# Two gates and two key projections regrouped into seven half-size products, and a scan begun on half its stacks

## Chip, cores and metric

The kernel runs on one core of one Trainium2 chip, in float32 throughout. The metric is the device time of one execution in microseconds (us), lower is better.

## What is computed

Two transformer blocks, one after the other, on 256 tokens of 1024 channels. The first mixes three branches (latent attention, gated linear attention, attention to a memory), each weighed by a gate, and ends in a feed-forward. The second mixes a state space branch and a dilated attention. Cut to what matters here:

```python
# first block
proj = rms_norm(x, g_mix) @ w_in                     # the last 3 * 1024 columns are gate_logits
gates = sigmoid(gate_logits + b_gate).reshape(B, S, 3, 1024)
y = gates[..., 0, :] * o_mla + gates[..., 1, :] * o_gla + gates[..., 2, :] * o_mem
x = x + y @ w_o
# second block: u_s, z_s, q, k, v, z_a, r_s, r_a = columns of rms_norm(x) @ w_in_2
q = rope(rms_norm(q))    # three groups of 512 columns, one per dilation
k = rope(rms_norm(k))    # the same
y_s = state_space(u_s)   # a scan along the tokens
y_a = dilated_attention(q, k, v)
m = sigmoid(r_s) * (...y_s...) + sigmoid(r_a) * (...y_a...)
```

## The kernel before

Every engine's program is written out by hand as one list. An engine does its list in order, and a semaphore wait holds back all that stands behind it on that engine.

**Jobs.** A projection of 512 columns is a job: both tiles of 128 tokens (its two halves), eight 128x128 by 128x512 products each. One such product is two MATMUL instructions in the trace. `fill` cuts a job into four parts of four products, to be laid between other work. Outputs take turns in two pairs of PSUM banks: before an output's first product TensorE waits until the output two places earlier has been taken out (`taken`, lines 195 to 204 and `half_job`).

**Groups of seven.** A projection of 1024 columns over 1024 channels can be a group (`GROUPS`): seven products of quarter blocks, Q1 to Q7, in place of eight, each four 128x512 products (`group_multiply`, L2028 and L2032). In exchange VectorE forms sums: four of the rows (`group_rows`; the row sums are shared where two groups have the same input), four of the weights, 128x2048 each (`group_t1`, `group_t3`, `group_t2`, `group_t4`), and five combinations of results (`group_z`, `group_v`, `group_c12`, `group_c22`, `group_last`). ScalarE copies Q1 and Q5 (`group_copy`) and takes out the first block (`group_first`). Of the waits: Q2 waits for the copy of Q1, Q6 for the third weight sum (T2), Q4 for the fourth (T4) and for `group_z`. The semaphore `first_out` counts `group_c12`; it stands for the first of a group's two PSUM pairs in `taken`.

**Weights** come through a ring of three 2 MB slots, loaded on SyncE's queue in the order of the jobs; a slot is freed by the last product that reads it (for a group: Q7 frees the first half's slot, Q4 the second's).

**The stretch of the gates** (L2156 on). After the latent attention, TensorE does products 2, 7, 3 of group MV (the memory's values), turns the normalised queries and keys of the memory attention (`turn`, L1892), does MV's Q6, waits for ScalarE to have taken the turned keys out (`is_turned("km")`), and enters a loop of nine steps. A step lays two parts of the gate jobs (in step 0 MV's Q4) ahead of: the memory attention's scores (L2167), their transposes, its values (L2183), and the lane products of one level of the gated linear attention (L2199). VectorE's step takes the scores and the values, takes the level's products, makes the decayed queries and keys and the exponents of the next level (`level_diff`), and from step 3 on takes and applies gates.

**The scan** (L2388 on). `us0` and `us1` of the state space branch come out of PSUM by ScalarE, VectorE stacks them with 16 copies (L1683), and eight steps of `drive` (L2381), VectorE's scan and `states` follow, with parts of eight jobs (`early`) between them.

**The dilated attention's queries and keys.** `dq0` to `dq2` and `dk0` to `dk2` are six jobs. Each goes through ScalarE (a copy and a square, L850 and L852), VectorE (`dqk`: sums, root, norm, rotation) and a transpose on TensorE. One buffer, `raw`, serves all six. Then come the groups RS, RA (the two output gates) and GLU, and the attention itself: `pair_scores` (L2444), VectorE's maxima (L1206), ScalarE's exponentials (L708), with eighths of RA and GLU laid between.

Of the kernel before, what the change touches and what calls it, by code (L numbers as in the profile page):

```python
# [12 lines left out]
P = 128  # L13
# [26 lines left out]
CH = 128  # L40
# [42 lines left out]
RG, MV, UP = 3, 4, 5  # L83
RS = UP + 4
# [4 lines left out]
def jobs_table():  # L89
# [13 lines left out]
    j = [(f"gate{i}", "w_in", C_GATE + 512 * i, 512) for i in (0, 1, 4, 5, 2, 3)]  # L103
# [10 lines left out]
    j += [(f"dk{g}", "w_in_2", C_DK + DW * g, DW) for g in range(NDIL)]  # L114
    out += [(n, n, w, 0, DM, c, m) for n, w, c, m in j]
    out += halves(RS, C_RS, "w_in_2") + halves(RA, C_RA, "w_in_2") + halves(GLU, 0, "w_glu_2")
# [10 lines left out]
ORDERS[UP] = ORDERS[WP] = (1, 2, 5, 7, 3, 6, 4)  # L127
# [3 lines left out]
ROWS = (0, 1, 1, 2, 3) + 4 * (4,) + (5, 5, 6, 7, 8)  # L131
# [6 lines left out]
for _job in JOBS:  # L138
# [10 lines left out]
BY_DVE = {"gg", "wo0", "wo1", "ao0", "ao1"} | {f"gate{i}" for i in range(6)}  # L149
# [30 lines left out]
    "dqk_rows": "one group's queries or keys of the dilated attention",  # L180
    "angle": "reduced rotary angles", "rope_ready": "ScalarE: cosines and sines",
# [19 lines left out]
    "u_ready": "state space inputs, even and odd steps stacked", "u2_ready": "halves of those stacks",  # L201
# [28 lines left out]
def act_at(i, n):  # L230

    return 3 * i + n - max(i - SO, 0)
# [12 lines left out]
def build(nc, d, out):  # L245
    with ExitStack() as ctx:
# [79 lines left out]
        sum_t2 = [r_gla, r_gla, r_gla, arena[:, dec_at:dec_at + 2048], arena[:, dec_at:dec_at + 2048]]  # L326
        sum_t3 = arena[:, r_at + 2048:r_at + 4096]
        sum_rows = [knT, mem_tok, mem_tok, arena[:, dec_at + 2048:dec_at + 4096], arena[:, dec_at + 2048:dec_at + 4096]]
# [47 lines left out]
        assert a4.at <= work_at  # L376
        tail_q1, tail_q5 = arena[:, 7680:8192], arena[:, 16384:16896]
        tail_t2 = {RS: m_tok, RA: sig_glu, GLU: m_tok, SO: arena[:, work_at:work_at + 2048], WP: arena[:, work_at + 4096:work_at + 6144]}
        rows_raw = arena[:, work_at + 6144:work_at + 8192]
        tail_rows = {RS: zs, RA: zs, GLU: rows_raw, SO: arena[:, work_at + 2048:work_at + 4096], WP: rows_raw}  # L380
# [25 lines left out]
        def group(i):  # L406
# [5 lines left out]
            if i < RS:  # L412
                t2, t3 = (x.rearrange("p (k n) -> p k n", n=512) for x in ((sum_t2[i], sum_t3) if i < UP else (up_t2, up_t3)))
                if i in (RG, MV):
                    t3 = b12
# [9 lines left out]
        def temporaries(i):  # L425
            if i >= RS:
                return tail_q1, tail_q5, tail_q5, tail_q1
            if i == MV:
                return copied_q1, across, across, copied_q1
            return (copied_q1, copied_q5, sum_z, sum_v) if i < UP else (up_q1, up_q5, up_z, up_v)  # L430
# [2137 lines left out]
```

## Time and profile before

| | us |
|---|---|
| median of 3 runs | 970.54 (969.59 to 970.54) |
| the profiled execution, whole | 969.14 |
| its span from first to last instruction | 967.2 |
| TensorE matmul, busy | 954.4 |
| VectorE, busy | 697.0 |
| ScalarE, busy | 220.4 |

The span leaves out some 1.9 us at the ends of the execution. All times in the views below are counted from the span's start. A line such as L928 is a helper that records all of VectorE's two-operand instructions, so operations are told apart by shape and place in time, not by line. In the chain of waits matmuls are shown from the end of the one before, in the timeline from their own issue, some 0.15 us earlier.

### The profile page before, as it was taken

How to read it: one execution, taken by the hardware profiler on the slowest of the kernel's cores; microseconds unless marked ns; L12 is line 12 of the kernel's file. 1: busy time of each engine (PE TensorE's matmuls, PEld its weight loads, DVE VectorE, ACT ScalarE, POOL GpSimd, SP SyncE). 2: the span in 40 equal slices, each digit the busy share in tenths (PEclk: the TensorE clock that was granted, in tenths of full speed). 3: DMA queues.
4: the chain of work that ended last, by engine and by line, in shares of the span. 5: the costliest groups of instructions: out<-in, count | busy, mean ns of one | idle time of the engine just before them, and what ended most of it. 6: DMA issues, size and time to landing. Idle time of an engine off the chain costs nothing.

```text
span 967.2 us, 12513 instructions
## 1 busy us (share of the span) xinstructions
PE 954.4 (99%) x5014; PEld 590.6 (61%) x5014; DVE 697.0 (72%) x1259; ACT 220.4 (23%) x438; POOL 23.2 (2%) x27
## 2 busy tenths in 40 slices
PE   7999999999999999999999999999999999999998
PEld 6944445754555449999844469458854444468544
DVE  4866964586566887866899763888965969674667
ACT  4313422223241232422200011001011321434200
POOL 0000000000002500000000000000000000000000
PEclk9999999999999999999999999999999999999999
DMA  9551731443345624344454443425243434321631
GB/s 329 149 196 43 283 130 44 174 134 128 97 158 155 182 109 169 115 175 175 174 174 173 174 149 124 164 88 175 87 138 124 173 116 150 109 105 45 218 130 44
DMA packets 53818, 139.76 MB, mean 144 GB/s; under 512 B 3968, under 2 KB 7904, under 8 KB 53760
## 3 DMA queue, kind: packets, MB, share of 16 engines
q1 hardware_dynamic: 52304, 135.07, 39.7%
q0 software_dynamic: 1248, 3.80, 1.7%
q8 instruction: 40, 0.66, 0.3%
q14 instruction: 18, 0.15, 0.0%
q10 hardware_dynamic: 208, 0.08, 0.0%
HBM read 137.90 MB, written 1.05 MB: 144 GB/s over the span
## 4 chain that ended last, share of the span: by engine, by line
PE 92%; DVE 5%; ACT 1%; issue 1%; DMA 0%; DVEq 0%; ACTq 0%
PE pair L1947 36%; PE pair L2032 18%; PE pair L2028 16%; PE pair L2286 6%; PE turned L1892 4%; PE score L2286 3%; DVE arena L928 3%; PE turned L2286 1%; PE score L2381 1%; PE score L2457 1%; PE score L2131 1%; PE score L2444 1%; PE score L2183 1%; PE score L2130 1%; PE score L2199 1%
## 5 line engine op out<-in xcount | busy, mean ns | idle before, releaser
L1947 PE MATMUL pair<-ring,hT 128*128 128x512 f32 (+2 forms) x640 | 269.8, 576 | 0.9 <-ACT hT L600 0.9
L928 DVE TENSOR_TENSOR arena<-arena 128x512 f32<-128x512 f32 (+6 forms) x329 | 194.1, 604 | 13.4 <-PE score L2286 4.1
L1947 PEld LDWEIGHTS pair<-ring,hT 128*128 128x128 f32 x640 | 119.2, 190 | 130.5 <-issue 125.5
L1947 PE MATMUL pair<-hT,ring 128*128 128x128 f32 (+2 forms) x464 | 76.4, 324 | 0.2 <-ACT hT L600 0.2
L928 DVE TENSOR_TENSOR arena<-pair,arena 128x512 f32<-128x512 f32 x57 | 39.4, 691 | 46.6 <-PE pair L2032 22.7
L2032 PE MATMUL pair<-ring,arena 128*128 128x512 f32 x160 | 71.7, 594 | 0.0
L1947 PEld LDWEIGHTS pair<-hT,ring 128*128 128x128 f32 (+1 forms) x464 | 66.0, 188 | 9.0 <-issue 1.3
L928 DVE TENSOR_TENSOR arena<-ring 128x2048 f32<-128x2048 f32 (+1 forms) x37 | 67.7, 1831 | 2.5 <-DMA ring<-in_w_ssm_out 1.3
L2032 PE MATMUL pair<-arena 128*128 128x512 f32 x144 | 65.3, 595 | 0.3 <-DVE arena L928 0.3
L2028 PE MATMUL pair<-arena 128*128 128x128 f32 x544 | 64.0, 276 | 0.0
L2032 PE MATMUL pair<-ring,hT 128*128 128x512 f32 x136 | 62.4, 598 | 0.8 <-DMA ring<-in_w_in 0.8
L2028 PEld LDWEIGHTS pair<-arena 128*128 128x128 f32 x544 | 62.2, 192 | 0.3 <-issue 0.2
L571 ACT ACTIVATE arena<-turned 128x512 f32<-128x512 f32 (+2 forms) x66 | 32.7, 536 | 129.2 <-PE turned L1892 129.2
L2028 PE MATMUL pair<-hT,ring 128*128 128x128 f32 x480 | 55.7, 275 | 0.0
L2028 PEld LDWEIGHTS pair<-hT,ring 128*128 128x128 f32 x480 | 54.7, 192 | 0.7 <-issue 0.5
L1892 PEld LDWEIGHTS turned<-ident,arena 128*128 128x128 f32 (+1 forms) x363 | 41.1, 141 | 22.2 <-issue 16.5
L1892 PE MATMUL turned<-ident,arena 128*128 128x128 f32 (+1 forms) x363 | 49.8, 275 | 1.7 <-ACT arena L571 0.7
L2032 PEld LDWEIGHTS pair<-ring,arena 128*128 128x128 f32 x160 | 29.7, 190 | 34.6 <-issue 34.6
L1206 DVE CUSTOM_DVE_ANT_0 arena<-score,masks 128x256 f32<-128x256 f32 (+2 forms) x40 | 18.0, 451 | 42.4 <-PE score L2131 22.1
L2032 PEld LDWEIGHTS pair<-arena 128*128 128x128 f32 x144 | 26.8, 190 | 32.0 <-issue 31.3
L2286 PE MATMUL pair<-ring,arena 128*128 128x512 f32 x96 | 43.5, 592 | 0.0
L928 DVE TENSOR_TENSOR arena<-arena,ring 128x2048 f32<-128x2048 f32 (+1 forms) x22 | 41.9, 1904 | 1.6 <-PE pair L2028 0.6
(221 smaller groups left out, 1004.4 us busy)
## 6 DMA issues: line engine op xcount, KB each, us to landing
ring<-in_w_in SPq DMA_DIRECT2D x33, 2048.0 KB, 8.4
ring<-in_w_up SPq DMA_DIRECT2D x8, 2048.0 KB, 8.5
ring<-in_w_down SPq DMA_DIRECT2D x8, 2048.0 KB, 7.8
ring<-in_w_o SPq DMA_DIRECT2D x4, 2048.0 KB, 7.9
ring<-in_w_mem_kv SPq DMA_DIRECT2D x2, 2048.0 KB, 7.8
ring<-in_w_glu SPq DMA_DIRECT2D x2, 2048.0 KB, 7.8
ring<-in_w_ssm_out SPq DMA_DIRECT2D x2, 2048.0 KB, 7.8
ring<-in_w_ukv SPq DMA_DIRECT2D x4, 512.0 KB, 3.7
```

The costliest lines, as they stand in the source:

```text
L571: act.activation(dst, src, ACT.Copy).then_inc(sem("turned_taken"), 1)
L928: return dve.tensor_tensor(o, a, b, op)
L1206: ins = dve.tensor_tensor_reduce(dst, src, mask, scale, -3e38, ALU.add, ALU.max, st[:, a:a + 1])
L1892: ins = pe.transpose(b[0:x.shape[1], a:a + rows], x, ident[0:rows, 0:rows])
L1947: ins = pe.matmul(o_, s, m, start=a, stop=b)
L2028: ins = pe.matmul(h[bank_][:, P * c:P * c + P], weights[:, k, P * c:P * c + P], rows[:, k, :], start=not onto and c == 0 and k == 0, stop= ...
L2032: ins = pe.matmul(h[bank_], rows[:, k, :], weights[:, k, :], start=not onto and k == 0, stop=k == 3, skip_group_check=True)
L2130: pe.matmul(o, qnT[:, SEQ * h + P * t:SEQ * h + P * t + P], knT[:, SEQ * h:SEQ * h + w], start=True, stop=False)
L2131: ins = pe.matmul(o, qpT[r, SEQ * (h // 2) + P * t:SEQ * (h // 2) + P * t + P], kpeT[r, 0:w], start=False, stop=True)
L2183: ins = pe.matmul(b[:, SEQ * t:SEQ * t + SEQ], s[:, 256 * t + P * k:256 * t + P * k + P], vm3[:, k, EV * h:EV * h + EV], start=k == 0, sto ...
L2199: ins = pe.matmul(b[lane0:lane0 + w, w * x:w * x + w], ks[:, P * x + k0:P * x + k0 + w], qs[:, P * x + q0:P * x + q0 + w], start=True, sto ...
L2286: ins = pe.matmul(product[q], rows[:, k, :], weights[:, k, :], start=g == 0 and k == 0, stop=g == 7 and k == 1, skip_group_check=True)
```

## The change

One more group, GT, takes the place of the jobs `gate0` and `gate1`, and one, DK, that of `dk1` and `dk2`.

- GT: its row sums are formed in step 8 of the attention before (`group_rows(GT)`); its seven products stand in steps 0 to 3 of the loop, its weight sums at the start of step 0 (T1), in step 1 (T3, T2), at the end of step 2 (T4 and `group_z`), and its last results at the end of step 3. Bias is added while the blocks are taken out. Both gates get one sigmoid and one multiplication.
- DK: seven products after `dk0`. Its row sums also serve RS and RA, whose own are gone. Two buffers, `raws`, take the place of `raw`; squares of the last two groups' keys are taken by ScalarE out of SBUF, and both share one root.
- The scan: of the 16 stacking copies VectorE keeps the first eight; ScalarE does the others. `drive(0)` moves ahead of the first two parts of `early`, and `states(7)` ahead of two parts at the end.

Of the diff, the parts that move work (further lines set buffers, names and places of temporaries; `stacks` lists the source and target of the eight copies of one half; `temporaries(GT)` and `(DK)` give their own scratch; `dqk_squares` and `dqk_turn` are `dqk` cut in two):

```diff
@@ -100,7 +101,8 @@
     out += [("mq", "mq", "w_in", 0, DM, C_MQ, 256), ("mk", "mk", "w_mem_kv", 0, DM, 0, 256)] + halves(MV, 256, "w_mem_kv")
-    j = [(f"gate{i}", "w_in", C_GATE + 512 * i, 512) for i in (0, 1, 4, 5, 2, 3)]
+    out += halves(GT, C_GATE)
+    j = [(f"gate{i}", "w_in", C_GATE + 512 * i, 512) for i in (4, 5, 2, 3)]
@@ -111,8 +113,9 @@
     j += [(f"dq{g}", "w_in_2", C_DQ + DW * g, DW) for g in range(NDIL)]
-    j += [(f"dk{g}", "w_in_2", C_DK + DW * g, DW) for g in range(NDIL)]
+    j += [("dk0", "w_in_2", C_DK, DW)]
     out += [(n, n, w, 0, DM, c, m) for n, w, c, m in j]
+    out += halves(DK, C_DK + DW, "w_in_2")
@@ -124,11 +127,11 @@
 ORDERS = {i: (1, 5, 2, 7, 3, 6, 4) for i in range(NG)}
-ORDERS[UP] = ORDERS[WP] = (1, 2, 5, 7, 3, 6, 4)
+ORDERS[GT] = ORDERS[UP] = ORDERS[WP] = (1, 2, 5, 7, 3, 6, 4)
...
-ROWS = (0, 1, 1, 2, 3) + 4 * (4,) + (5, 5, 6, 7, 8)
+ROWS = (0, 1, 1, 2, 3, 4) + 4 * (5,) + (6, 6, 6, 7, 8, 9)
@@ -758,12 +780,21 @@
                     level_exp(i)
+                if i == 1:
+                    group_copy(GT, 5)
...
                     exps("mem", i, ((0, 256, 0), (256, 256, 1)))
-                if i in (4, 6, 8):
-                    gate_sigmoid((i - 4) // 2)
+                if i == 0:
+                    group_copy(GT, 1)
+                if i == 4:
+                    act.wait_ge(sem("first_out"), GT + 1)
+                    act.wait_ge(sem("second_out"), GT + 1)
+                    act.wait_ge(sem("last_out"), GT + 1)
+                    act.activation(gate_buf, gate_buf, ACT.Sigmoid).then_inc(sem("gate_sig"), 1)
+                if i == 8:
+                    gate_sigmoid(2)
@@ -816,6 +847,10 @@
                 ins.then_inc(sem("taken_act"), 1)
+            act.wait_ge(sem("taken_act"), taken("us1")[1])
+            for h, jj, s, src, dst in stacks(1):
+                ins = act.activation(dst, src, ACT.Copy)
+            ins.then_inc(sem("u2_late"), 1)
@@ -837,30 +872,43 @@
-            for n in range(6):
-                name = f"dq{n}" if n < 3 else f"dk{n - 3}"
-                act.wait_ge(sem("z_silu"), 3)
-                if n:
-                    for _k in range(2):
-                        turned((qdT if n - 1 < 3 else kdT)[:, 1024 * ((n - 1) % 3) + 512 * _k:1024 * ((n - 1) % 3) + 512 * _k + 512], 512)
-                if n == 0:
-                    act.wait_ge(sem("h_ready"), 4 * 8)
+            def turned_dqk(n):
...
+                for k in range(2):
+                    turned((qdT if n < 3 else kdT)[:, 1024 * (n % 3) + 512 * k:1024 * (n % 3) + 512 * k + 512], 512)
...
+            act.wait_ge(sem("z_silu"), 3)
+            act.wait_ge(sem("h_ready"), 4 * 8)
+            for n, name in enumerate(("dq0", "dq1", "dq2", "dk0")):
+                x, squares = raws[n % 2]
...
                 for t in range(2):
-                    act.activation(raw[:, 512 * t:512 * t + 512], p[:, 512 * t:512 * t + 512], ACT.Copy)
+                    act.activation(x[:, 512 * t:512 * t + 512], p[:, 512 * t:512 * t + 512], ACT.Copy)
                 for t in range(2):
-                    ins = act.activation(raw2[:, 512 * t:512 * t + 512], p[:, 512 * t:512 * t + 512], ACT.Square)
+                    ins = act.activation(squares[:, 512 * t:512 * t + 512], p[:, 512 * t:512 * t + 512], ACT.Square)
                 ins.then_inc(sem("taken_act"), 1)
-                if n == 2:
+                if n == 0:
...
                                        scale=1.5957691216057308).then_inc(sem("gelu_sig"), 1)
+                else:
+                    turned_dqk(n - 1)
+            group_copy(DK, 1)
+            group_copy(DK, 5)
+            turned_dqk(3)
+            group_first(DK, raws[1][0][:, 0:512])
+            act.wait_ge(sem("first_out"), DK + 1)
+            act.wait_ge(sem("second_out"), DK + 1)
+            act.activation(raws[0][1], raws[0][0], ACT.Square).then_inc(sem("dk_squared"), 1)
+            act.wait_ge(sem("group_act"), act_at(DK, 3))
+            act.wait_ge(sem("last_out"), DK + 1)
+            act.activation(raws[1][1], raws[1][0], ACT.Square).then_inc(sem("dk_squared"), 1)
...
             group_first(RS, by_tokens(rsig)[0])
-            for k in range(2):
-                turned(kdT[:, 2048 + 512 * k:2048 + 512 * k + 512], 512)
+            turned_dqk(5)
+            turned_dqk(4)
@@ -983,15 +1031,17 @@
                 weights_in(f"g{i}x")
-                if i and i != RA:
-                    dve.wait_ge(sem("group_product"), product_at(i - 1 if i != GLU else RS, 6))
+                if i == GT:
+                    dve.wait_ge(sem("group_product"), product_at(MV, 4))
+                elif 0 < i < DK or i in (SO, WP):
+                    dve.wait_ge(sem("group_product"), product_at(i - 1, 6))
...
                 weights_in(f"g{i}y")
-                if 0 < i < RS:
+                if 0 < i < DK:
@@ -1277,6 +1327,7 @@
                     m_squares(0)
+                    group_rows(GT)
@@ -1335,9 +1386,17 @@
             level_diff(0)
+            gt4 = by_tokens(gate_buf)
+            h, (_, _, z, v), biased = group(GT)[0], temporaries(GT), ckv[:, 0:512]
             for i in range(9):
+                if i == 0:
+                    group_t1(GT)
...
                     group_last(MV, vm4[2])
+                    group_t3(GT)
+                    dve.wait_ge(sem("bgate0"), 16)
+                    dve.wait_ge(sem("group_product"), product_at(GT, 2))
+                    link(tt(gt4[0], h[1], bgate[:, 0:512], ALU.add))
@@ -1387,10 +1446,25 @@
                         mark(dve.tensor_copy(am3[q, :, q], ad3[q]), "amat")
-                if i in (3, 5, 7):
-                    gate_take((i - 3) // 2)
-                if i in (5, 7):
-                    gate_apply((i - 5) // 2, (i - 5) // 2 + 1)
+                if i == 1:
+                    group_t2(GT)
+                if i == 2:
+                    group_t4(GT)
+                    group_z(GT)
+                if i == 3:
+                    group_v(GT)
+                    dve.wait_ge(sem("bgate1"), 16)
+                    link(tt(biased, v, bgate[:, 512:1024], ALU.add))
+                    dve.wait_ge(sem("group_product"), product_at(GT, 3))
+                    mark(tt(gt4[1], h[3], biased, ALU.add), "first_out")
+                    mark(tt(gt4[3], z, biased, ALU.add), "second_out")
+                    link(tt(v, v, bgate[:, 0:512], ALU.subtract))
+                    group_last(GT, gt4[2])
+                if i == 5:
+                    dve.wait_ge(sem("gate_sig"), 1)
+                    link(tt(o_mla, o_mla, gate_buf, ALU.mult))
+                if i == 7:
+                    gate_take(2)
@@ -1404,8 +1478,8 @@
             mark(tt(o_gla, o_gla, r_gla, ALU.mult), "mixer_out")
-            gate_apply(2, 3)
-            gate_apply(3, 4)
+            gate_apply(2, 2)
+            gate_apply(3, 3)
@@ -1672,16 +1749,18 @@
-            u4 = uT.rearrange("p (m c s) -> p m c s", c=CH, s=2)
-            v4 = u2.rearrange("p (m h c) -> p m h c", h=2, c=CH)
-            for i in range(2):
-                dve.wait_ge(sem("taken_act"), taken(f"us{i}")[1])
-                for h in range(2):
-                    for jj in range(2):
-                        for s in range(2):
-                            q, r = 64 * h + 32 * jj, 64 * jj + 32 * s
-                            ins = dve.tensor_copy(v4[r:r + 32, 4 * i:4 * i + 4, h, :], u4[q:q + 32, 4 * i:4 * i + 4, :, s])
-                            step(ins) if (h, jj, s) != (1, 1, 1) else mark(ins, "u2_ready")
+            def dqk(n):
...
+                x, squares = raws[n % 2]
+                dqk_squares(n, squares, 192)
+                mean(st[:, 192:208], st[:, 192:208], DD)
+                inverse_root(192, 16)
+                dqk_turn(n, x, squares, 208)
...
+            dve.wait_ge(sem("taken_act"), taken("us0")[1])
+            for h, jj, s, src, dst in stacks(0):
+                ins = dve.tensor_copy(dst, src)
+                step(ins) if (h, jj, s) != (1, 1, 1) else mark(ins, "u2_ready")
@@ -1721,31 +1800,42 @@
                     z_silu(("zs0", "zs1", "za")[m - 5])
-            dqk(0)
             ssm_out(7)
-            dqk(1)
...
                 mark(tt(z, z, y, ALU.mult), "gelu_z")
-            dqk(2)
+            dqk(0)
+            group_rows(DK)
...
                 link(tt(z, y, zs[:, 1024 * i:1024 * i + 1024], ALU.mult))
-            group_rows(RS)
+            dqk(1)
+            group_t1(DK)
+            dqk(2)
+            group_t3(DK)
             dqk(3)
+            group_t2(DK)
+            group_t4(DK)
             group_t1(RS)
-            dqk(4)
+            group_z(DK)
+            group_middle(DK, raws[0][0][:, 0:512], raws[0][0][:, 512:1024])
+            group_last(DK, raws[1][0][:, 512:1024])
             group_t3(RS)
-            dqk(5)
+            dqk_squares(5, raws[0][1], 192)
+            dqk_squares(4, raws[1][1], 208)
+            mean(st[:, 192:224], st[:, 192:224], DD)
+            inverse_root(192, 32)
+            dqk_turn(5, raws[0][0], raws[0][1], 224)
             group_t2(RS)
+            dqk_turn(4, raws[1][0], raws[1][1], 240)
...
             group_z(RS)
+            dve.wait_ge(sem("turned_ready"), T_DQK)
             group_t1(RA)
-            dve.wait_ge(sem("turned_ready"), T_DQK)
@@ -2156,10 +2246,13 @@
             for i in range(9):
-                if i:
-                    fill(["gate0", "gate1", "gate4", "gate5"], i - 1, 2)
+                if i < 4:
+                    for g, q in (((MV, 4), (GT, 1)), ((GT, 2), (GT, 5)), ((GT, 7), (GT, 3)), ((GT, 6), (GT, 4)))[i]:
+                        group_multiply(g, q)
+                elif i < 7:
+                    fill(["gate4", "gate5"], i - 4, 2)
                 else:
-                    group_multiply(MV, 4)
+                    fill(["gate4", "gate5"], i - 1, 1)
@@ -2388,18 +2481,20 @@
             pe.wait_ge(sem("ca_ready"), 2)
-            fill(early, 0, 2)
             for m in range(8):
-                if m in (0, 4):
-                    pe.wait_ge(sem("u2_ready"), m // 4 + 1)
+                if m == 0:
+                    pe.wait_ge(sem("u2_ready"), 1)
+                if m == 4:
+                    pe.wait_ge(sem("u2_late"), 1)
                 drive(m)
-                fill(early, 3 * m + 2, 1)
-                fill(early, 3 * m + 3, 1)
+                fill(early, 3 * m, 1)
+                fill(early, 3 * m + 1, 1)
...
                     states(m - 1)
-                fill(early, 3 * m + 4, 1)
+                fill(early, 3 * m + 2, 1)
+            fill(early, 12, 2)
+            states(7)
             fill(early, 13, 2)
-            states(7)
@@ -2407,19 +2502,26 @@
                 for k in range(2):
-                    turn(f"dqk{n}", ktiles(raw, DW)[4 * k:4 * k + 4])
+                    turn(f"dqk{n}", ktiles(raws[n % 2][0], DW)[4 * k:4 * k + 4])
             pe.wait_ge(sem("ssm_taken"), 8)
-            for n, name in enumerate(("dq2", "dk0", "dk1", "dk2")):
+            for n, name in enumerate(("dq2", "dk0")):
...
                 job(name)
+            turn_dqk(2)
+            for q in (1, 5, 2):
+                group_multiply(DK, q)
+            turn_dqk(3)
+            for q in (7, 3, 6, 4):
+                group_multiply(DK, q)
+            for q in (1, 5, 2, 7):
+                group_multiply(RS, q)
             turn_dqk(4)
-            for q in (1, 5, 2, 7):
+            for q in (3, 6):
...
             assert n_unit["turned"] == T_DQK, n_unit
-            for q in (3, 6, 4):
-                group_multiply(RS, q)
+            group_multiply(RS, 4)
...
             eighths = [0]
```

## Rows read from the trace of the kernel before

**Rows 1.** The page: busy time by engine, and the chain's shares by engine
```profile
PE 954.4 (99%) x5014; PEld 590.6 (61%) x5014; DVE 697.0 (72%) x1259; ACT 220.4 (23%) x438; POOL 23.2 (2%) x27
...
PE 92%; DVE 5%; ACT 1%; issue 1%; DMA 0%; DVEq 0%; ACTq 0%
```

**Rows 2.** Windows: stretch, busy time of each engine, clock, DMA share, GB/s
```profile
210.00:305.00 95.00, 95.00 (x692) 50.46 (x691) 62.01 (x108) 28.61 (x41) 1.61 (x3) 1.00 0.42 135
...
720.00:815.00 95.00, 95.00 (x295) 44.83 (x294) 70.46 (x144) 22.05 (x41) 0.00 (x0) 1.00 0.42 151
```

**Rows 3.** Chain of waits: a whole job; start, us, what
```profile
751.48 13.74 PE pair L1947 x32
```

**Rows 4.** Groups by form: VectorE's operations, busy us, mean ns
```profile
L928 DVE TENSOR_TENSOR arena<-arena 128x1024 f32<-128x1024 f32 x43 | 51.9, 1223 | 1.2
L928 DVE TENSOR_TENSOR arena<-ring 128x2048 f32<-128x2048 f32 x21 | 48.1, 2292 | 1.9 <-DMA ring<-in_w_ssm_out 1.3
...
L928 DVE TENSOR_TENSOR arena<-pair,arena 128x512 f32<-128x512 f32 x57 | 39.4, 691 | 46.6 <-PE pair L2032 22.7 <-PE pair L2028 17.1 <-PE pair L1947 5.5
```

**Rows 5.** Chain of waits: TensorE through steps 0, 2 and 3 of the loop
```profile
216.92 6.87 PE pair L2032 x16
223.78 1.06 PE score L2167 x4
224.84 0.69 PE score L2199 x50
...
245.76 0.63 PE score L2199 x32
...
256.82 0.69 PE score L2199 x50
```

**Rows 6.** Timeline, ScalarE: silu's sigmoid, turned queries and keys, exponentials
```profile
217.29 1.06 ACT L738 ACTIVATE arena<-arena 128x1024 f32<-128x1024 f32 x1 [9.22 <-DVE arena L928]
218.26 1.07 ACT L571 ACTIVATE arena<-turned 128x512 f32<-128x512 f32 x2
...
227.93 0.19 ACT L708 ACTIVATION_READ_ACCUMULATOR arena<-arena,stats 128x1 f32 x1
```

**Rows 7.** Timeline, VectorE: steps 0, 2 and 3 of the loop
```profile
199.27 2.29 DVE L928 TENSOR_TENSOR ring<-ring 128x2048 f32<-128x2048 f32 x1
...
225.89 0.42 DVE L1206 CUSTOM_DVE_ANT_0 arena<-score,masks 128x256 f32<-128x256 f32 x1
...
247.99 3.81 DVE L928 TENSOR_TENSOR arena<-arena 128x1024 f32<-128x1024 f32 x4
...
258.61 3.21 DVE L928 TENSOR_TENSOR arena<-arena 128x256 f32<-128x256 f32 x5
```

**Rows 8.** Timeline, VectorE: one of the keys' `dqk`, first scores of the dilated attention
```profile
783.50 1.22 DVE L1659 TENSOR_REDUCE stats<-arena 128x16 f32<-128x1024 f32 x1 [3.69 <-ACT arena L852]
...
787.05 1.22 DVE L928 TENSOR_TENSOR arena<-arena,stats 128x1024 f32<-128x1024 f32 x1
...
790.50 0.62 DVE L928 TENSOR_TENSOR arena<-arena 128x128 f32<-128x128 f32 x2
...
822.10 0.69 DVE L1206 CUSTOM_DVE_ANT_0 arena<-score,masks 128x512 f32<-128x512 f32 x1
```

**Rows 9.** Timeline, TensorE: first and second `pair_scores` of the dilated attention
```profile
820.15 1.14 PE L2444 MATMUL score<-arena 64*128 64x256 f32 x8
...
823.68 0.70 PE L2444 MATMUL score<-arena 64*128 64x256 f32 x4 [0.48 <-DVE stats L1206]
```

**Rows 10.** Timeline, VectorE and TensorE: second stacking copies, first drive
```profile
603.19 3.56 DVE L1683 COPY arena<-arena 32x512 f32<-32x512 f32 x8 [3.59 <-ACT arena L815]
...
608.76 1.16 PE L2381 MATMUL score<-arena 64*128 64x128 f32 x16
```

**Rows 11.** Timeline, TensorE: the first matmuls of the kernel
```profile
5.25 4.02 PE L2039 MATMUL score<-ident 128*128 128x128 f32 x20 [5.25 <-DMA ident<-in_c_ident]
```

**Rows 12.** Windows: the first two us of those matmuls, columns as above
```profile
5.00:7.00 2.00, 1.75 (x8) 1.75 (x9) 0.59 (x4) 1.75 (x3) 0.00 (x0) 1.00 1.02 336
```

**Rows 13.** Chain of waits: eight transposes a little later
```profile
14.48 0.88 PE turned L1892 x8
```

## What I expect before seeing the result

> **What bounds the kernel now.** I read the page first. TensorE is busy for 99% of the span and is 92% of the chain that ended last [rows 1]; VectorE has a quarter of the span free. The windows then say whether that average holds where the change works: in both stretches TensorE is busy without a gap, while VectorE does 62.0 us of 95 in the one with the gates and 70.5 of 95 in the one with the queries and keys [rows 2]. So a product less is worth its full time, if no wait takes its place. That second half cannot be read from shares: VectorE's spare time lies in pieces, between results that it waits for. So I read the chain and the timeline of the two stretches instruction by instruction, and laid the new order over them. "Done" below is a time on the trace of before.
>
> **What is removed.** A job of 16 products is 32 MATMULs and 13.74 us [rows 3], so four products are 3.43 us. A group does in 28 products what two jobs do in 32: GT and DK save 3.43 us each, 6.9 us together. If all else hid, the profiled execution would go from 969.1 to 962.3 us.
>
> **What is added to VectorE.** A weight sum of 2048 columns is 2.29 us, an operation out of PSUM 0.69 us [rows 4]; with the 0.03 us between them I count 2.32 and 0.72. Row sums are 4 x 0.72 = 2.9 us. GT adds all of these, DK shares its row sums with RS. None of it is on the path by itself; what counts is when each piece is due.
>
> **GT, four waits.**
> (a) The row sums (2.9 us) go into a stretch where VectorE runs without a pause from 199.3 us [rows 7] until past 217 us. There ScalarE's second silu sigmoid waits for VectorE, and behind it on ScalarE stand the turned queries and keys, done at 219.3 us [rows 6]. TensorE wants them at the end of MV's Q6, 216.92 + 3.43 = 220.35 us [rows 5]. The slack is 1.0 us, the delay 2.9: TensorE waits 1.9 us.
> (b) TensorE then does MV's Q4 (3.43), GT's Q1 (3.43), scores and lanes (1.75) [rows 5]: from 222.25 to 230.9 us. Next is Q2, which waits for ScalarE's copy of Q1. That copy stands behind the exponentials of head 0, these behind VectorE's maxima, and these now behind 2.9 us of row sums and 2.3 us of T1: they begin at 225.9 + 5.2 = 231.1 us [rows 7]. Before, the exponentials ended at 228.1 us [rows 6], so 2.2 us after the maxima began; a copy of 0.6 us more gives 233.9 to 234.0. TensorE waits 3.1 us.
> (c) In step 2, TensorE's lane products end at 246.4 us [rows 5], and only then can VectorE do its level, which ends at 247.99 + 3.81 = 251.8 us [rows 7], 5.4 us later. In the new order T4 and `group_z` follow that: 5.4 + 2.3 + 0.7 = 8.5 us after the lane products. TensorE has Q6 (3.43 us) to do before Q4 wants both. It waits 5.0 us. This is independent of (a) and (b), since VectorE waits for TensorE in each step anyhow.
> (d) In step 3 the lane products end at 257.5 us [rows 5] and VectorE's level at 261.8 us [rows 7], 4.3 us later. Then come `group_v`, the biased V and the block that posts `first_out`, 3 x 0.72 = 2.2 us. TensorE has nothing between: its next item, the first part of `gate4`, needs that PSUM pair and so `first_out`. It waits 6.5 us. Before, the same pair was free long ahead.
> Together 1.9 + 3.1 + 5.0 + 6.5 = 16.5 us of waits, against 3.4 saved: **+13.1 us**. Steps 7 and 8 now carry one part (3.43 us) in place of two. A level takes VectorE 5.4 us at most from lane products to the next exponents, of which the decayed operands are the first part, so I count 0.3 us there, bounds 0 and 2. What follows the loop keeps its order.
>
> **DK.** I lay TensorE out from the end of `dk0`, which is due where `dk0` was, at 765.2 us (751.48 + 13.74, [rows 3]). A transpose pair is 0.9 us. Turn, Q1, Q5, Q2: 776.4. The fourth `dqk` is ready by then: before, its first sum began 3.5 us after its job's end and it lasted 7.6 us [rows 8], so 776.3 at the latest. Turn, Q7, Q3, Q6: 787.6; Q4: 791.0. RS's Q1, Q5, Q2, Q7, a turn, Q3, Q6, a turn: 813.4; Q4: 816.8. Before, RS ended at the first scores, 820.3 us by the chain [rows 9]: 3.43 us earlier, as it should be.
> VectorE over the same time: after DK's Q6 (787.6, 0.25 us for the signal) three combinations end at 790.0; the last block waits for Q4 and ends at 792.0; RS's T3 794.3; two sums of squares at 1.25 and one root (2.3, from 784.7 to 787.05 us in [rows 8]) 799.1; rotation of one group (787.05 to 791.1 in [rows 8], 4.1) 803.2; T2 805.5; rotation of the other 809.7; T4 812.0; `group_z` 812.7. So far TensorE's deadlines (turn 804.7, Q6 809, turn 812.5, Q4 813.4) hold. But RA's T1 now stands behind the wait for the last turn, at 813.4: T1 815.8, GLU's row sums 818.6, RS's middle 820.8, RA's T3 823.1, RS's last block 823.9. Only then come the first maxima of the dilated attention, which began at 822.1 us before [rows 8]. RS's `first_out` comes at some 820.1, so RA's Q1 waits too. The second `pair_scores` started at 823.7 us, right behind those maxima [rows 9], and starts 1.7 us later now. From there the order is that of before. So 3.4 us saved become **+1.7 us**: 5.1 us of new waits. Bounds: -3.4 us if VectorE catches up during the attention, +4 if the weight loads or ScalarE's squares come late as well (RS's second half is loaded some 8 us after Q7, at 789, and wanted at 792).
>
> **The scan.** The stacking copies take VectorE 3.6 us a half; the second half ended at 606.8 us, and the first `drive` began at 608.8 [rows 10]. Moving two parts (6.9 us) from ahead of it to behind changes the order of TensorE's work and not its amount. The wait for the first half is over well before; ScalarE's eight copies have four steps of some 13 us until they are due. I cost it at nothing; without that cover it would cost the copies' 3.6 us. As TensorE was not waiting there, it gains nothing either.
>
> **The clock.** The first 20 matmuls, after 5.25 us of idleness, took 4.02 us, 0.20 each [rows 11], in a window granted 1.00 of 2.4 GHz by the record [rows 12]; transposes of the same size took 0.11 soon after [rows 13]. So 1.9 us went there at what looks like the half rate. The waits (c) and (d) are about as long, so each may be followed by such a loss: 0 to 3.7 us in all. I take one, 1.9 us. The Trainium skill, "TensorE: Matmul & The Clock Gate", section "HAM oscillation — how this bites in real kernels", says that long idle gaps send the clock to its lower level and that this is paid anew each time; by it (c) and (d) would both pay. The spacing above agrees, the granted clock of the same window does not.
>
> **Sum.** 969.1 + 13.1 + 0.3 + 1.7 + 1.9 = 986.1 us for a profiled execution. The median of the runs lies 1.4 us above that execution: **987 us**, 1.7% slower.
>
> **Rivals.**
> Hidden after all (chance 0.07): VectorE's sums come in time and the 6.9 us stay, 970.5 - 6.9 = 963.7 us. For it speak VectorE's 33 free us in the first stretch [rows 2]. It needs T4 and `group_z` done within the 3.43 us of Q6 after step 2's lane products; by rows 5 and 7 they come 8.5 us after. It decides if VectorE does them ahead of its level.
> About even (0.03): GT's waits come to some 7 us only, because (c) and (d) overlap with time in which TensorE would wait anyway: 969 to 972. Against it: TensorE has no such time there [rows 2].
> Half of it (0.13): the steps of GT hold, but (a) or (b) is absorbed and DK keeps its gain, 972 to 980 us.
> My forecast (0.67): 980 to 992, with no, one or two losses of clock.
> Worse (0.10): (b) too is followed by slow matmuls, or RS's weights are late and DK costs 4 us or more: 992 to 998.
> The range 977 to 992 leaves out 0.1 above and about as much below. A measurement of this kernel tells 0.2% (1.9 us) from no change: faster 0.07, the same 0.03, slower 0.90.
>
> **What the new profile would show.** TensorE's idle time, 13 us before, should be near 35. Its waits should name VectorE ahead of the line L2032 or its successor (Q4, 5 us), ahead of the first part of `gate4` (6.5 us), ScalarE ahead of Q2 (3 us) and ahead of MV's Q4 (2 us). Before the second `pair_scores` there should be 3 us on VectorE, before RA's Q1 2 us. No wait at `drive`. I would be wrong if the loop of nine steps were not about 13 us longer than before: then I have misread what stands before what on VectorE.

## The result, and the profile after

The changed kernel takes **994.12 us** (median of 4, 992.89 to 995.22), the kernel before 970.07 us beside it (969.54 to 970.54). The ratio is 1.0249, interval 1.0236 to 1.0262: 2.5% slower. The sign was foreseen. The size was not: 987 us was forecast and the range ended at 992. The profiled execution took 994.16 us, its span 992.4 us, against 969.14 and 967.2 before; the difference to explain is 25.2 us of span. One of the 11 executions of `e1_scan_only` below took 2556.51 us, and its ratio leaves that one out.

The page of the changed kernel, busy times and the chain that ended last (answering [rows 1]):

```profile
PE 955.9 (96%) x4998; PEld 590.6 (60%) x4998; DVE 719.2 (72%) x1260; ACT 224.1 (23%) x442; POOL 23.5 (2%) x27
...
PE 86%; DVE 11%; ACT 2%; issue 1%; DMA 0%; DVEq 0%; ACTq 0%
```

TensorE is idle for 992.4 - 955.9 = 36.5 us, and VectorE's share of the chain has risen from 5 to 11%. A second thing stands in the same row: TensorE is busy 1.5 us longer than before, though it does 6.9 us less work. Some of its matmuls have become slower.

Its windows over the two stretches of [rows 2], same columns:

```profile
210.00:305.00 95.00, 78.65 (x500) 39.89 (x499) 61.49 (x97) 22.46 (x36) 1.07 (x2) 0.93 0.32 103
720.00:815.00 95.00, 95.00 (x330) 46.18 (x329) 68.46 (x122) 20.67 (x36) 0.00 (x0) 1.00 0.40 143
```

The stretch of the gates has 16.35 us of idle TensorE and a granted clock of 0.93; the one with the queries and keys is as full as before.

What TensorE waited for (us in total, times, longest):

```profile
PE pair L2122 <- DVE arena L976: 7.7, 3, 5.0
PE pair L2037 <- DVE arena L976: 6.6, 1, 6.6
PE score L2129 <- DMA ident<-in_c_ident: 5.2, 1, 5.2
PE score L2546 <- DVE stats L1256: 3.7, 2, 3.3
PE pair L2122 <- ACT arena L635: 2.8, 1, 2.8
...
PE pair L2122 <- ACT arena L593: 1.9, 1, 1.9
```

L2122 is the group's product (L2032 before), L2037 that of a job, L2546 `pair_scores`, L976 VectorE's two-operand helper (L928 before). Of these only the 5.2 us at the kernel's start and 0.9 of the 3.7 us at `pair_scores` were there before. Where these waits stand, and what follows each, is in TensorE's timeline of the loop (start, length, count; the bracket is the idle time ahead):

```profile
217.27 3.60 PE L2122 MATMUL pair<-arena 128*128 128x512 f32 x8
222.80 3.70 PE L2122 MATMUL pair<-ring,arena 128*128 128x512 f32 x8 [1.93 <-ACT arena L593]
...
234.50 5.37 PE L2122 MATMUL pair<-ring,hT 128*128 128x512 f32 x8 [2.82 <-ACT arena L635]
239.70 3.60 PE L2122 MATMUL pair<-arena 128*128 128x512 f32 x8
...
265.69 5.31 PE L2122 MATMUL pair<-ring,hT 128*128 128x512 f32 x8 [4.98 <-DVE arena L976]
...
281.70 9.27 PE L2037 MATMUL pair<-ring,hT 128*128 128x512 f32 x16 [6.63 <-DVE arena L976]
...
293.77 7.13 PE L2037 MATMUL pair<-ring,hT 128*128 128x512 f32 x16
```

The brackets are the four waits (a) to (d) of the prediction: 1.93, 2.82, 4.98 and 6.63 us. The second column shows the rest. Eight matmuls take 3.60 us; behind (b) and (c) the same eight take 5.37 and 5.31, and behind (d) sixteen take 9.27 in place of 7.13. Behind (a) they take their usual time. The windows over these matmuls name the cause; the granted clock is the third number from the end:

```profile
234.50:239.70 5.20, 5.20 (x8) 2.19 (x9) 4.40 (x5) 1.06 (x1) 0.00 (x0) 0.67 0.01 3
239.70:243.20 3.50, 3.50 (x9) 1.33 (x7) 0.69 (x1) 0.00 (x0) 0.00 (x0) 1.00 0.02 5
265.70:270.90 5.20, 5.20 (x8) 2.03 (x8) 0.00 (x0) 0.00 (x0) 0.00 (x0) 0.68 0.00 0
281.70:290.80 9.10, 9.10 (x16) 3.87 (x17) 1.97 (x3) 0.00 (x0) 1.07 (x2) 0.76 0.20 58
```

0.67, 0.68 and 0.76 are means of a part at 1.2 GHz and a part at 2.4 GHz: inside the last of them, windows of 1.3 us show 0.50 up to 285.6 us, and 1.00 stands from 287.0 us on. The product right after the first slow one, at 239.7 us, is at 1.00 again. So each of the three waits is paid twice: as idleness, and as 1.8, 1.7 and 2.1 us of slow matmuls behind it.

At the dilated attention (answering [rows 9]):

```profile
836.73 1.13 PE L2546 MATMUL score<-arena 64*128 64x256 f32 x8
...
840.24 1.96 PE L2122 MATMUL pair<-ring,hT 128*128 128x512 f32 x4 [2.38 <-DVE arena L976]
...
845.49 0.91 PE L2546 MATMUL score<-arena 64*128 64x256 f32 x4 [3.29 <-DVE stats L1256]
846.32 3.43 PE L2122 MATMUL pair<-ring,hT 128*128 128x512 f32 x4
```

Two waits in a row, with only 1.96 us of work between them. The four matmuls behind the first wait still take their usual time, at a granted clock of 1.00; the four behind the second take 3.43 us, nearly twice as long, at 0.56. With the scores between them (0.91 for 0.70) the slow part costs 1.7 us. The first maxima began at 843.91 us by VectorE's timeline.

**The ledger.** Start: the first 20 matmuls took 4.57 us against 4.02 [rows 11], +0.5. Saved products, -6.9. Waits (a) to (d) and a small one of 0.45 us later in the loop, +16.8. Slow matmuls behind them, +5.6. New waits at the dilated attention, 2.38 + 3.29 - 0.48 = +5.2, slow matmuls there +1.7. The output's last transfers are issued 23.5 us later than before, and the span ends 3.7 us after them in place of 2.0: +1.7. That is 24.6 of 25.2 us. The last item stands out: in the nine other profiles of this study the end came 2.0 to 2.6 us after the last issue. Whether it belongs to this execution alone is not shown, for the other three runs of the changed kernel took 992.89 to 995.22 us and were on the whole no shorter.

### The profile page after: what moved, and what is told of

Read it like the earlier page. It is cut to its first block, busy times and chain, and to the rows that moved or that the text cites. A ratio compares the mean times of both kernels' runs of the same rounds, so it can differ in the third digit from the quotient of the medians.

```text
span 992.4 us, 12510 instructions
## 1 busy us (share of the span) xinstructions
PE 955.9 (96%) x4998; PEld 590.6 (60%) x4998; DVE 719.2 (72%) x1260; ACT 224.1 (23%) x442; POOL 23.5 (2%) x27
## 4 chain that ended last, share of the span: by engine, by line
PE 86%; DVE 11%; ACT 2%; issue 1%; DMA 0%; DVEq 0%; ACTq 0%
PE pair L2037 30%; PE pair L2122 19%; PE pair L2118 15%; DVE arena L976 6%; PE pair L2379 6%; PE turned L1982 3%; PE score L2379 3%; PE turned L2379 1%; DVE ring L976 1%; PE score L2474 1%; PE score L2546 1%; PE score L2559 1%; PE score L2221 1%; PE score L2220 1%; PE turned L2461 0%
## 5 line engine op out<-in xcount | busy, mean ns | idle before, releaser
L2037 PE MATMUL pair<-ring,hT 128*128 128x512 f32 (+2 forms) x512 | 215.7, 576 | 7.5 <-DVE arena L976 6.6
L976 DVE TENSOR_TENSOR arena<-arena 128x256 f32<-128x256 f32 (+6 forms) x332 | 196.7, 607 | 15.8 <-PE score L2379 4.1
L2037 PEld LDWEIGHTS pair<-ring,hT 128*128 128x128 f32 x512 | 96.1, 192 | 110.7 <-issue 105.8
L2122 PE MATMUL pair<-ring,hT 128*128 128x512 f32 x184 | 88.8, 626 | 11.0 <-DVE arena L976 7.4
L2122 PE MATMUL pair<-ring,arena 128*128 128x512 f32 x192 | 85.9, 594 | 1.9 <-ACT arena L593 1.9
L2122 PE MATMUL pair<-arena 128*128 128x512 f32 x176 | 79.8, 595 | 0.3 <-DVE arena L976 0.3
L976 DVE TENSOR_TENSOR arena<-pair,arena 128x512 f32<-128x512 f32 x60 | 41.5, 692 | 52.8 <-PE pair L2122 29.3
L2037 PE MATMUL pair<-hT,ring 128*128 128x128 f32 (+2 forms) x464 | 76.2, 324 | 0.2 <-ACT hT L622 0.2
L976 DVE TENSOR_TENSOR arena<-ring 128x2048 f32<-128x2048 f32 (+1 forms) x39 | 72.3, 1854 | 3.7 <-DMA ring<-in_w_ssm_out 1.7
L2037 PEld LDWEIGHTS pair<-hT,ring 128*128 128x128 f32 (+1 forms) x464 | 66.0, 188 | 8.6 <-ACT hT L622 1.0
L2122 PEld LDWEIGHTS pair<-ring,hT 128*128 128x128 f32 x184 | 35.1, 200 | 52.2 <-issue 45.1
L2118 PEld LDWEIGHTS pair<-arena 128*128 128x128 f32 x544 | 62.2, 192 | 0.3 <-issue 0.2
L2122 PEld LDWEIGHTS pair<-ring,arena 128*128 128x128 f32 x192 | 35.5, 190 | 43.7 <-issue 40.8
L2122 PEld LDWEIGHTS pair<-arena 128*128 128x128 f32 x176 | 32.8, 190 | 39.3 <-issue 38.2
L1982 PEld LDWEIGHTS turned<-ident,arena 128*128 128x128 f32 (+1 forms) x363 | 41.1, 141 | 22.2 <-issue 16.5
L1256 DVE CUSTOM_DVE_ANT_0 arena<-score,masks 128x256 f32<-128x256 f32 (+2 forms) x40 | 18.1, 452 | 45.0 <-PE score L2221 22.1
L976 DVE TENSOR_TENSOR arena<-arena,ring 128x2048 f32<-128x2048 f32 (+1 forms) x24 | 46.5, 1936 | 1.7 <-PE pair L2118 0.6
```

The lines of the kernel that those rows point to most:

```text
L976: return dve.tensor_tensor(o, a, b, op)
L1256: ins = dve.tensor_tensor_reduce(dst, src, mask, scale, -3e38, ALU.add, ALU.max, st[:, a:a + 1])
L1982: ins = pe.transpose(b[0:x.shape[1], a:a + rows], x, ident[0:rows, 0:rows])
L2037: ins = pe.matmul(o_, s, m, start=a, stop=b)
L2118: ins = pe.matmul(h[bank_][:, P * c:P * c + P], weights[:, k, P * c:P * c + P], rows[:, k, :], start=not onto and c == 0 and k == 0, stop= ...
L2122: ins = pe.matmul(h[bank_], rows[:, k, :], weights[:, k, :], start=not onto and k == 0, stop=k == 3, skip_group_check=True)
```

## The experiments

Two theories stood at the start. Mine: order alone; TensorE waits for results queued too late on VectorE and ScalarE, and each long wait is followed by a spell of TensorE's lower clock. The rival: the seven-product form costs time by itself here, through VectorE's added sums.

### One part alone: the scan, the keys

`e1_scan_only` is the kernel before with the change at the scan and nothing else; `e2_keys_only` has the scan and DK, with the gates as jobs.

```
e1:  -fill(early, 0, 2)      (ahead of the first drive)
     +stacks(1) on ScalarE, "u2_late" waited for at m == 4
     states(7) ahead of the last parts, as in the change
e2:  e1, and DK in place of dk1, dk2; gate0, gate1 stay jobs
```

> The kernel before with the scan's part of the change alone (half of the stacking copies on ScalarE, first drive two parts earlier, states(7) two parts earlier). Theory: TensorE does the same work and waits for nothing there, so 970.1 us, within 0.2% of the kernel before, and no wait of TensorE at drive. Rival: the earlier scan takes load off VectorE where it is late and gains 2 us or more (968 us or less). Second rival: the last gate of the scan's stretch (za) comes 2 to 3 us late and stalls TensorE: 972 to 973 us.

> The change without GT: the two gates are jobs as before, the keys are the group DK and the scan is as changed. Theory: 3.4 us saved, 5.2 us of new waits at the first pair_scores (2.4 before RA's Q1, 3.3 before the second pair_scores, 0.5 of it there before), and some 1.7 us of matmuls at half rate behind them: 970.1 + 3.5 = 973.5 us. Rival, by which the waits were inherited from the late gates: DK gains its 3.4 us, 966.7 us.

e1: 970.79 us, ratio 1.0007 (0.9998 to 1.0016), and no wait at `drive`. The scan's part does nothing that can be told. e2: 973.92 us, ratio 1.0042 (1.0028 to 1.0056), close to the 973.5 expected: with DK, which should save 3.4 us, the kernel is 3.9 us slower. TensorE's timeline of e2 at the dilated attention:

```profile
821.03 2.64 PE L2082 MATMUL pair<-ring,hT 128*128 128x512 f32 x4 [2.39 <-DVE arena L962]
826.28 1.23 PE L2503 MATMUL score<-arena 64*128 64x256 f32 x4 [2.60 <-DVE stats L1240]
827.43 3.78 PE L2082 MATMUL pair<-ring,hT 128*128 128x512 f32 x4
```

The same two waits as in the full change (the second is 2.60 us in place of 3.29), without GT: they belong to DK. Slow matmuls stand behind them again, so the forecast's +1.7 us lacked this loss. Here they begin behind the first wait already: 2.64 us for 1.96, then 1.23 for 0.70, 3.78 for 1.98, and 1.53 for the 0.94 of the next scores. Together that is 3.6 us, where the full change lost 1.7 in the same place. What is left of the 24 us, some 20, is GT's.

### The waits filled with matmuls

In `e3_kept_busy` the waits stay, but TensorE spends most of them on products of the identity with a mask whose result nobody reads: 3 ahead of GT's Q2, 5 ahead of its Q4, 7 ahead of `gate4`, 2 and 3 at the dilated attention. Nothing of the computation is changed.

```diff
+                        if (g, q) == (GT, 2):
+                            keep_busy(3)
+                        if (g, q) == (GT, 4):
+                            keep_busy(5)
                         group_multiply(g, q)
                 elif i < 7:
+                    if i == 4:
+                        keep_busy(7)
...
```

> The changed kernel with idle TensorE time filled: before GT's Q2, before GT's Q4, before the first part of gate4, before RA's Q1 and before the second pair_scores stand 3, 5, 7, 2 and 3 extra 128x128 by 128x512 products into a free bank (0.86 us each, results unused). They fit into the waits and release nothing. Theory that idleness brings the half rate: the waits stay (seen as extra matmuls), the slow stretches behind them go back to 3.6, 3.6, 7.1 and 2.0 us, and the kernel gets 6 to 7.5 us faster than the changed one: 994.1 - 7 = 987 us. Rival, that the stretches are slow for what they read or for load elsewhere: 994 us, or more by what the products overrun.

985.82 us (985.52 to 986.32), ratio 1.0165 (1.0151 to 1.0179): 8.3 us less than the changed kernel, by adding work, and more than the 6 to 7.5 us expected. TensorE's timeline:

```profile
232.09 2.84 PE L1981 MATMUL turned<-masks,ident 128*128 128x512 f32 x6
234.97 3.67 PE L2129 MATMUL pair<-ring,hT 128*128 128x512 f32 x8
...
259.32 4.46 PE L1981 MATMUL turned<-masks,ident 128*128 128x512 f32 x10
...
264.47 3.67 PE L2129 MATMUL pair<-ring,hT 128*128 128x512 f32 x8 [0.69 <-DVE arena L976]
...
272.13 6.28 PE L1981 MATMUL turned<-masks,ident 128*128 128x512 f32 x14
...
278.83 7.11 PE L2044 MATMUL pair<-ring,hT 128*128 128x512 f32 x16 [0.42 <-DVE arena L976]
```

The groups behind (b), (c) and (d) are back at 3.67, 3.67 and 7.11 us, and their windows are granted the full clock:

```profile
234.90:238.40 3.50, 3.46 (x9) 1.63 (x9) 3.36 (x5) 1.06 (x1) 0.00 (x0) 1.00 0.02 6
264.50:268.10 3.60, 3.60 (x9) 1.41 (x9) 0.00 (x0) 0.00 (x0) 0.00 (x0) 1.00 0.02 5
278.80:285.70 6.90, 6.87 (x16) 3.10 (x17) 2.00 (x3) 0.00 (x0) 1.06 (x2) 1.00 0.24 78
```

The page's span is 984.1 us, of which the output's landing is 2.1 us in place of 3.7. Up to the output's issue the trace is 6.7 us shorter, although its start took 0.5 us longer (the turn ahead of MV's Q6 begins at 216.86 us against 216.40). Those 7.2 us are what the ledger gives to slow matmuls, 5.6 + 1.7 = 7.3 us. The idle time and its second cost are so told apart: the second is the clock's.

### The waits taken away by order

`e4_results_early` is the changed kernel with VectorE's late pieces moved ahead of work that nobody waits for yet: T4 from the end of step 2 to the end of step 1, `group_z` and the block of `first_out` ahead of the memory attention's scores in steps 2 and 3. `e5_rows_copy_early` moves the row sums out of the crowded step 8 to its start, and ScalarE's copy of Q1 ahead of head 0's exponentials. `e6_gates_on_time` has both.

```diff
 e4, VectorE's step of the loop
+                if i == 2:
+                    group_z(GT)
+                if i == 3:
+                    group_v(GT)
+                    ...
+                    mark(tt(gt4[1], h[3], biased, ALU.add), "first_out")
                 if i < EH:
...
                 if i == 1:
                     group_t2(GT)
+                    group_t4(GT)
...              (no longer at the ends of steps 2 and 3)
 e5, VectorE, step 8 of the attention before
+                if h == 8:
+                    group_rows(GT)
                 if h >= 2:
...
                     m_squares(0)
-                    group_rows(GT)
 e5, ScalarE's step of the loop
+                if i == 0:
+                    group_copy(GT, 1)
                 if i < EH:
                     exps("mem", i, ((0, 256, 0), (256, 256, 1)))
-                if i == 0:
-                    group_copy(GT, 1)
```

> The changed kernel with only VectorE's order altered: T4 moves to the end of step 1, group_z to the start of step 2, and the blocks that post first_out to the start of step 3, all ahead of that step's scores. Theory: the waits before Q4 (5.0 us) and before gate4 (6.6 us) go and with them two slow stretches (1.7 and 2.1 us): 994.1 - 15.4 = 978.7 us, up to 1 us more because scores are taken later. Rival, that GT's extra work is too much for VectorE in these steps wherever it stands: the waits come back at the values or the lane products, 988 us or more.

> The changed kernel with only the first two waits treated: GT's row sums stand ahead of head 6's values in step 8 of the attention, where VectorE waited 3.5 us for TensorE, and ScalarE copies Q1 ahead of head 0's exponentials. Theory: the waits before MV's Q4 (1.9 us) and before GT's Q2 (2.8 us) go, and the slow stretch behind the second (1.8 us): 994.1 - 6.5 = 987.6 us. Rival, that they are covered by the later waits, since VectorE sets the pace anyhow: 993 to 994 us.

> Both VectorE/ScalarE reorderings of the gates together (four waits treated), keys as changed. Theory: all four waits of 16.4 us and their three slow stretches of 5.6 us go: 994.1 - 22 = 972.1 us; counted from before, 970.1 - 3.4 (GT) + 3.9 (DK as measured alone) = 970.6 us. I expect 970.5 to 972.5. Rival, that GT itself costs what the group saves (weights late in the ring, scores late): 974 us or more.

| | median us | ratio | against the changed kernel, each counted from the kernel before beside it |
|---|---|---|---|
| e4 | 978.78 | 1.0094 (1.0080 to 1.0108) | -15.3 |
| e5 | 986.77 | 1.0184 (1.0169 to 1.0199) | -7.0 |
| e6 | 971.70 (12 runs) | 1.0012 (1.0001 to 1.0022) | -22.1 |

The kernel before had 970.07 us beside the changed kernel, 970.05 beside e4 and 969.73 beside e5 and e6. The waits (c) and (d) and their slow matmuls come to 4.98 + 6.63 + 1.7 + 2.1 = 15.4 us, and e4 gives back 15.3. For (a) and (b) it is 1.93 + 2.82 + 1.8 = 6.6, and e5 gives 7.0. The two add up (22.3 against 22.1), as they should if the waits are independent. Agreement to 0.1 us is in part luck: the loss at the dilated attention, left as it was in all three, is not the same in their profiles (below). TensorE's timeline of e4 shows which are gone and that (b) keeps its price:

```profile
234.99 5.37 PE L2123 MATMUL pair<-ring,hT 128*128 128x512 f32 x8 [2.82 <-ACT arena L635]
...
261.04 3.60 PE L2123 MATMUL pair<-ring,hT 128*128 128x512 f32 x8
...
268.64 7.13 PE L2038 MATMUL pair<-ring,hT 128*128 128x512 f32 x16
```

In e5 the other two are left whole, by its list of waits:

```profile
PE pair L2123 <- DVE arena L976: 7.8, 3, 5.0
PE pair L2038 <- DVE arena L976: 6.6, 1, 6.6
```

VectorE does the same sums in all of them. So the rival theory falls: the sums cost nothing where their place is right. What e6 has left are DK's waits, 2.39 us ahead of RA's Q1 and 3.2 in all at `pair_scores`:

```profile
818.25 2.43 PE L2124 MATMUL pair<-ring,hT 128*128 128x512 f32 x4 [2.39 <-DVE arena L976]
823.50 1.23 PE L2548 MATMUL score<-arena 64*128 64x256 f32 x4 [2.81 <-DVE stats L1256]
824.65 3.78 PE L2124 MATMUL pair<-ring,hT 128*128 128x512 f32 x4
```

As in e2, the matmuls are slow from the first wait on, and the loss is 3.5 us with the scores that follow; in e4 it is 3.9. In the changed kernel and in e5 the same wait of 2.38 or 2.39 us had nothing slow behind it, and the loss was 1.7. So one and the same wait can have this cost or not, from one profile to the next. The 12 runs of e6 lie in two clusters, 967.7 to 969.8 and 971.4 to 973.0 us. The five of the lower one all have a mean granted clock of 0.998; of the seven of the upper one five have 0.994 to 0.996 and two 0.998. The clock may so be a part of what divides them, which is not shown: the one profile is of the upper cluster.

### Both parts on time

`e7_all_on_time` is e6 with DK's consequences mended on VectorE: RS's middle results ahead of the wait for the last turn, RA's T3 behind the next maxima, GLU's row sums later still. `e8_keys_on_time` is e2 with the same edit, so e7 without GT.

```diff
             group_z(RS)
-            dve.wait_ge(sem("turned_ready"), T_DQK)
-            group_t1(RA)
-            group_rows(GLU)
             rs4, ra4, glu4 = by_tokens(rsig), by_tokens(asig), by_channels(sig_glu)
             group_middle(RS, rs4[1], rs4[3])
-            group_t3(RA)
+            dve.wait_ge(sem("turned_ready"), T_DQK)
+            group_t1(RA)
             group_last(RS, rs4[2])
...              (steps of the attention, behind the maxima)
+                    if s == 0:
+                        group_t3(RA)
...
                     group_c22(RA, ra4[3])
+                    group_rows(GLU)
```

> As the one before, and behind the keys VectorE forms RS's middle before it waits for the last turn, RA's T3 behind the second pair of maxima, and GLU's row sums one step of the attention later. Theory: the two waits before the second pair_scores go and the group DK gets its 3.4 us: 970.1 - 6.9 = 963.2 us, 963 to 966 with what the moved sums cost in steps 0 and 1. Rival, that VectorE is full there and the moved work returns as waits in the next step: 967 us or more.

> Gates as jobs like before, DK and the scan as changed, with the reordering behind the keys. Theory: 970.1 - 3.4 = 966.7 us, up to 1.5 us more for the moved sums. Rival: 970 us or more, if VectorE is full there.

e7: **965.08 us** (964.72 to 966.37), ratio 0.9956 (0.9944 to 0.9968). It beats the kernel before by 0.4%, little but clear of the interval, with the seven-product groups in. e8: 968.26 us (11 runs), ratio 0.9985 (0.9976 to 0.9993). Between the two lies GT alone, 3.2 us, of the 3.43 that its four products are worth. The page and the longest waits of e7:

```profile
PE 948.3 (98%) x4998; PEld 588.4 (61%) x4998; DVE 719.2 (75%) x1260; ACT 224.1 (23%) x442; POOL 23.3 (2%) x27
```

```profile
PE score L2132 <- DMA ident<-in_c_ident: 5.4, 1, 5.4
PE score L2549 <- DVE stats L1256: 1.8, 2, 1.4
...
PE turned L1985 <- DVE arena L1873: 0.9, 1, 0.9
```

TensorE's busy time is 955.9 - 948.3 = 7.6 us below that of the changed kernel, for the same 4998 matmuls: the slow ones are gone. The two waits of 1.8 and 0.9 us were 0.9 and 0.4 before, so some 1.4 us of DK's 3.4 are still lost, to the second `pair_scores` of the attention's third step and to a turn. The sum 969.73 - 6.86 + 1.4 = 964.3 us (from the median before on that chip) is 0.8 us short of what was measured.

## Why the prediction was right in kind and short in size

- **The loop's waits, +16.5 us.** Right one by one: 1.9, 3.1, 5.0, 6.5 were forecast, 1.93, 2.82, 4.98, 6.63 came. They were had by laying each engine's list out in time from the durations of [rows 3 to 7]; VectorE's 33 free us of [rows 2] gave no hint of them. e4 and e5 took two each away by order alone.
- **Steps 7 and 8, 0.3 us.** One wait of 0.45 us, at the end of the loop. The sign named for being wrong was a loop not about 13 us longer. It was 19.5 us longer (it ended 20.0 us later, and the start had taken 0.5), though nothing on VectorE was misread: 5.6 us of the excess are slow matmuls, which the sign had not allowed for.
- **DK.** The waits came as forecast: 5.2 us of new waits against 5.1, with the first maxima at 843.91 us, where the forecast's 823.9 and the 20.0 us by which the loop had ended late (325.65 against 305.66 us) put them. As a term it was short, since the waits were priced without the clock's loss behind them. Its working has one small slip: before, the `dqk` at 783.50 us begins 3.7 us after its job's end at 779.8 and not 3.5, which moves nothing.
- **The scan, nothing.** Right (e1).
- **The clock, 1.9 us: the step that failed.** The forecast said that (c) and (d) "may" each be followed by a loss, "0 to 3.7 us in all. I take one, 1.9 us." Four spells came, at 1.8, 1.7, 2.1 and 1.7 us, together **7.3 us**. The price of one was right for this profile; at the attention it is 3.5 to 3.9 us in those of e2, e4 and e6. Their number was not: (b), with 2.8 us, and the pair of waits at the attention were long enough too. I had measured against the one wait that the trace of before showed with slow matmuls behind it, 5.25 us [rows 11], took only waits of that length, and halved even those because the window there was recorded at 1.00 [rows 12]. The Trainium skill, "TensorE: Matmul & The Clock Gate", section "HAM oscillation — how this bites in real kernels", has the clock's loss paid anew after each long gap. The trace of the changed kernel agrees, with losses behind (b), (c), (d) and the pair. By it the forecast would have had 988 to 989 us for (c) and (d) alone.
- **The rest**, 1.7 us of output landing and 0.5 us at the start, was in no forecast. With 7.3 for 1.9 the sum for a profiled execution is 991.5 us, and with these two 993.7, against 994.16 measured. The step from there to the median did not hold either: 1.4 us was to be added (986.1 + 1.4 is 987.5, written as 987), and the median of the changed kernel, 994.12, is that of its profiled execution.
- **The rival "Worse"** (992 to 998 us, 0.10) had it: (b) too was followed by slow matmuls. That alone would not have reached its range: three losses in place of one, 5.6 us for 1.9, make 989.8 us for a profiled execution. The fourth, behind DK's waits, stood in no rival as such. I gave this one too little, for want of asking which of my own waits were shorter than 5 us and might still count.
- **The chances.** The range was said to leave out about 0.1 below. The two rivals under 972 us have 0.10 already, and a part of the third's 0.13 (972 to 980) lies under 977 too, so more than 0.1 was left out below.

## What to carry to other kernels

When work is taken off the engine that sets the time, lay out when each result it needs will be ready on the other engines' lists; a free quarter of an engine says nothing of that. Price a new TensorE wait of the lengths seen here (2.8 us and more) at itself plus the slow matmuls behind it, each time anew, and one of 2.4 us as perhaps so. And before dropping a change whose sums come late, move them: here 22 of 24 us were gone with the gates' few lines, and the rest turned into a gain.

## What was not expected of the hardware

In the changed kernel the lower clock came after waits of 2.82, 4.98 and 6.63 us and after one of 3.29 us (with 2.38 us of idleness and 1.96 us of work right before it), and not after one of 1.93 us. A wait of 2.4 us was followed by it in e2, e4 and e6 (four matmuls in 2.64, 3.19 and 2.43 us) and not in the changed kernel and e5 (1.96 and 1.95). Behind the single waits of 2.82, 4.98 and 6.63 us a spell cost 1.8, 1.7 and 2.1 us, so hardly more behind the longest, and behind the pair it cost 1.7 to 3.9 us from one profile to another. Forty matmuls that compute nothing, laid in the waits, made the kernel 8.3 us faster, 6.7 of them ahead of the output's last transfers. The kernel's first matmuls run at half their later speed in a window that the record shows at 1.00 [rows 11, 12]; that stays unexplained.
